# Values, gates and matrix memory as two stages, and the second modulation moved into the feature stages

## What is computed

```python
h = modulate(rmsnorm(x), shift, scale)          # shift, scale: 2 of 6 blocks of silu(c) @ ada_w + ada_b
P = h @ w_in                                    # RWKV, qk, values, i and f gates, ...
# mLSTM, per direction z (2), head (4) and chunk, state C, n, m:
b = cumsum(fc); m_new = max(b_end + m, max(b_end - b + ic))
C = exp(b_end + m - m_new) * C + sum_s w_end[s] * v[s] k[s]^T
s = (q @ k.T) * exp(log_d - m_row)              # log_d masked: causal within the chunk
h = (s @ v + a_inter * C q) / max(|den|, exp(-m_row))
y = sum over z of h * rsqrt(mean(h^2)) * norm_g
# then RWKV-7 (features, scan) for context and latent tokens, merge, experts
```

## Time and profile before

| | us |
|---|---|
| median of 3 runs (lowest, highest) | 3045.11 (3043.85, 3045.47) |
| the profiled execution: its time, its span | 3045.84, 3044.1 |
| values stage, gates stage, mLSTM stage | 75.0, 83.1, 170.0 |
| context features, latent features | 34.9, 53.8 |
| PE busy in the span | 2727.3 (90%) |
| granted clock in the span | 0.924 |

### The profile page before, as it was taken

The page is one execution under the profiler, slowest core; times in us unless marked ns, Lnnn a source line. Parts: engine busy times, 40 slices in busy tenths (PEclk is TensorE's granted clock), DMA queues, the critical chain, the costliest instruction groups (busy, mean ns, idle before and its releaser), DMA issues. The chain is left out here.

```text
span 3044.1 us, 54577 instructions
## 1 busy us (share of the span) xinstructions
PE 2727.3 (90%) x20260; PEld 2215.5 (73%) x20260; DVE 1279.3 (42%) x2767; ACT 1043.2 (34%) x1778; POOL 779.4 (26%) x641
## 2 busy tenths in 40 slices
PE   5798899678599959969978999997999999999998
PEld 2684268476499748748857888886888888888886
DVE  1221313454655533228994444442003444444443
ACT  2221113424333422233215666663223222222222
POOL 0520100032244224334445555552441000000000
PEclk9899965589799979989998999998999999999999
DMA  4220410000000033223323554455444555555552
GB/s 169 83 62 31 173 56 1 7 1 9 2 0 0 5 111 96 90 82 115 100 66 122 186 196 162 174 208 199 145 144 169 193 193 192 193 193 193 193 192 80
DMA packets 159929, 349.08 MB, mean 115 GB/s; under 512 B 13224, under 2 KB 79272, under 8 KB 156528
## 3 DMA queue, kind: packets, MB, share of 16 engines
q1 hardware_dynamic: 159856, 348.10, 33.3%
HBM read 276.75 MB, written 71.30 MB: 114 GB/s over the span
## 5 line engine op out<-in xcount | busy, mean ns | idle before, releaser
L85 PE MATMUL ps_a<-h_hi,u_hi 128*128 128x512 f32 x1024 | 407.1, 398 | 23.3 <-PEq L105 16.6
L86 PE MATMUL ps_a<-h_hi,u_lo 128*128 128x512 f32 x1024 | 400.9, 391 | 0.0
L87 PE MATMUL ps_a<-h_lo,u_hi 128*128 128x512 f32 x1024 | 400.4, 391 | 0.0
L2389 DVE TENSOR_TENSOR v_lo<-v_raw,v_hi 128x1024 fp32r<-128x1024 f32 x128 | 158.2, 1236 | 564.5 <-ACT v_hi L2347 564.4
L85 PE MATMUL ps_y<-gated_hi,v_hi 128*128 128x512 f32 x768 | 299.6, 390 | 3.1 <-DVE gated_lo L2391 3.1
L2347 ACT ACTIVATE v_hi<-v_raw 128x1024 fp32r<-128x1024 f32 x128 | 135.8, 1061 | 478.1 <-PE ps_a L87 469.7
L87 PE MATMUL ps_y<-gated_lo,v_hi 128*128 128x512 f32 x768 | 299.4, 390 | 0.0
L86 PE MATMUL ps_y<-gated_hi,v_lo 128*128 128x512 f32 x768 | 299.3, 390 | 0.0
L85 PEld LDWEIGHTS ps_a<-h_hi,u_hi 128*128 128x128 f32 x1024 | 193.9, 189 | 62.4 <-issue 23.0
L87 PEld LDWEIGHTS ps_a<-h_lo,u_hi 128*128 128x128 f32 x1024 | 193.5, 189 | 40.9
L86 PEld LDWEIGHTS ps_a<-h_hi,u_lo 128*128 128x128 f32 x1024 | 193.8, 189 | 37.9
(11 more groups left out here) (473 smaller groups left out, 5653.1 us busy)
## 6 DMA issues: line engine op xcount, KB each, us to landing
u_raw<-in_uT SPq DMA_DIRECT2D x128, 512.0 KB, 3.6
v_raw<-in_v SPq DMA_DIRECT2D x128, 512.0 KB, 4.8
a_scratch<-act SPq DMA_DIRECT2D x128, 256.0 KB, 2.2
w_scratch<-w_block SPq DMA_DIRECT2D x8, 4096.0 KB, 12.1
w_ring<-w_scratch SPq DMA_DIRECT2D x64, 512.0 KB, 4.4
gated<-a_scratch SPq DMA_DIRECT2D x128, 256.0 KB, 4.8
ada_ring<-in_ada_w SPq DMA_DIRECT2D x12, 2048.0 KB, 7.6
mg_raw<-in_w_merge SPq DMA_DIRECT2D x36, 512.0 KB, 3.5
```

Source lines behind the costliest of these rows:

```text
L85: pe.matmul(out, wh, xh, start=first, stop=False)
L86: pe.matmul(out, wl, xh, start=False, stop=False)
L87: return pe.matmul(out, wh, xl, start=False, stop=last)
L2389: v.tensor_tensor(vl[:, q], v_raw[:, q], vh[:, q], ALU.subtract).then_inc(v_lo, 1)
```

## The change

- The gates stage is gone. `phase_values` now loads the gate weights first, multiplies both kinds of gates in one product of 100 columns (`F_ROW` = 64), and runs the gate chain on DVE and ACT while PE makes four value tiles; the turning of the rows stands between the fourth and the fifth tile.
- `phase_mlstm` works on two heads a unit (8 context units, 16 latent ones). Scores are made once for both directions, 512 wide; the exponents are 512 wide; keys are turned once for both directions. In the first part, per head, these stand beside the context units; in the second only three pairs of products stand in a unit. Half of the queries-by-state pair uses array rows 0 to 63, half 64 to 127; half of the keys-by-values pair makes output rows 0 to 63, half 64 to 127. The sum of squares goes from DVE to ACT, in blocks of 8 instructions a chunk, and one direction's last scaling to POOL.
- The 8 modulation tiles go to the feature stages: 3 with the context, 5 with the latent tokens, after the norm's sums, which now wait for all of ACT's reads of the four banks they share. ACT copies the first tile's row ahead of the norm's Ln.
- h of the latent tokens is kept in `mixed` (`b.acc`), so some instructions of the modulation stage that were 768 wide are now 512 and 256; POOL's two adds a tile in the projection become one copy.
- The semaphores are cleared once more, behind the mLSTM.

```diff
+MOD_SECOND = MOD_FIRST + 3
...
+                for s, part in enumerate((xx[:, j], h[:, j, TX:])):
+                    m = act.activation(part, part, ACT.Identity, bias=b.mod[:, j, s:s + 1])
                 m.then_inc(shifted, 1)
                 act.wait_ge(shifted, j + 1)
-                act.activation(b.hh[:, j], h[:, j], ACT.Copy).then_inc(rounded, 1)
+                act.activation(b.hh[:, j, 0:TX], xx[:, j], ACT.Copy)
+                act.activation(b.hh[:, j, TX:], h[:, j, TX:], ACT.Copy).then_inc(rounded, 1)
...
-        ps = [ctx.enter_context(nc.psum_tensor(f"ps_rf{k}" + tag, [P, 512], F32)) for k in range(8)]
+        ps = [ctx.enter_context(nc.psum_tensor(f"ps_rf{k}" + tag, [P, 512], F32)) for k in range(4)]
+        mod = Modulation(nc, ctx, a, b, "_2" + tag, lo, hi, sb("mod_row" + tag, [2, hi - lo, MOD_W]), 3)
...
+            mod.load_bias(sp)
+            for n in range(n_mod):
+                mod.load(sp, n)
...
+            mod.copy_row(act, 0)
...
             pe.wait_ge(sq_done, 1)
+            pe.wait_ge(a_done, 2 * PAIRS)
             for c in range(PAIRS):
-                mm = pe.matmul(ps[4 + c][:, 0:T], b.block_ones[:], tmp[:, c, :], start=True, stop=True)
+                mm = pe.matmul(ps[c][:, 0:T], b.block_ones[:], tmp[:, c, :], start=True, stop=True)
             mm.then_inc(norm_mm, 1)
+            for n in range(n_mod):
+                mod.multiply(pe, n)
+            mod.turn(pe)
...
+        def _(pe):
+            pe.wait_ge(w_in, 16)
+            for j in range(KT):
+                pe.matmul(ps_x[0:F_ROW + GROWS, :], wg[:, j, :], b.h[:, j, 0:TX], start=(j == 0), stop=(j == KT - 1))
+            for j in range(KT):
+                mm = pe.matmul(ps_c[0:F_ROW + GROWS, 0:TC], wg[:, j, :], b.h[:, j, TX:],
+                               start=(j == 0), stop=(j == KT - 1))
+            mm.then_inc(g_mm, 1)
+            pe.wait_ge(v_in, 16)
+            def value(t):
...
+                for j in range(KT):
+                    mm = pe.matmul(ps_v[t % 2][:], b.h[:, j, t * MC:(t + 1) * MC], wv[:, j, :], start=(j == 0), stop=(j == KT - 1))
+                mm.then_inc(v_mm, 1)
+            for t in range(early_v):
+                value(t)
+            pe.wait_ge(rows_done, 1)
+            for n in range(NCH):
+                for k in range(4):
+                    o = (n * 2 + k % 2) * GROWS
+                    tr = pe.transpose(ps_t[k // 2][:, o:o + GROWS], turn[:, k, n * MC:(n + 1) * MC], ident[:])
+            tr.then_inc(t_done, 1)
+            for t in range(early_v, n_v):
+                value(t)
...
+                act.wait_ge(v_mm, t + 1)
+                act.activation(b.vM[:, t, :, 0:DV], ps_v[t % 2][:].rearrange("p (h v) -> p h v", v=DV),
+                               ACT.Copy).then_inc(v_out, 1)
+            for t in range(2):
+                evict(t)
             act.wait_ge(want[1], 1)
+            act.activation(rows[:, 4], rows[:, 4], ACT.Exp).then_inc(act_done, 1)
             act.activation(rows[:, INTER], rows[:, INTER], ACT.Exp).then_inc(act_done, 1)
             act.activation(rows[:, FLOOR], rows[:, FLOOR], ACT.Exp, scale=-1.0).then_inc(act_done, 1)
-            act.activation(rows[:, 4], rows[:, 4], ACT.Exp).then_inc(act_done, 1)
-            for n in range(2, n_mod):
-                mod.copy_row(act, n)
+            for t in range(2, n_v):
+                evict(t)
...
+            def scores(h):
+                j, lo = h // 2, h % 2 * DQK
+                if h < 2:
+                    pe.wait_ge(kc_done, 2)
+                else:
+                    pe.wait_ge(p_done, 2 * (h - 1))
+                for i in range(n_x):
+                    t = slice(i * MC, (i + 1) * MC)
+                    mm = pe.matmul(ps_s[h % 2][:, t], b.qX[lo:lo + DQK, HP + j, t], b.qX[lo:lo + DQK, j, t],
...
+            def exponent(h, z):
+                n = 2 * h + z
+                out = ps_e[(n + 1) % 2]
+                if n == 0:
+                    pe.wait_ge(kept, 1)
+                elif n % 4 == 1:
+                    pe.wait_ge(kx_done, n // 4 * 2 + 2)
+                    if n > 1:
+                        pe.wait_ge(exp_done, (n - 1) * n_x)
+                else:
+                    pe.wait_ge(exp_done, (n - 1) * n_x)
+                wide = mask[:, z].unsqueeze(1).to_broadcast([P, n_x, MC])
+                pe.matmul(out[:].rearrange("p (n t) -> p n t", t=MC), b.ident[:], wide, start=True, stop=False)
+                pe.matmul(out[:], select[:, z * MH + h, :], b.neg_m[:], start=False, stop=True).then_inc(e_mm, 1)
...
+                v0 = chunk if latent else n_x + chunk
+                kw = (kw_x if latent else kw_c)[:, z, j, chunk]
+                if latent:
+                    t = slice(chunk * MC, (chunk + 1) * MC)
+                    if i == 0:
+                        pe.wait_ge(p_done, 2 * (2 * j + 1) + z + 1)
+                    if n >= per:
+                        pe.wait_ge(c_done, n - per + 1)
+                    for p in range(2):
+                        pe.matmul(ps_u[k][:, p * W:(p + 1) * W], pw[:, z, 2 * j + p, t], b.vM[:, v0, 2 * j + p, :],
                                   start=True, stop=True)
-                    else:
-                        act_s.wait(pe, 0, f"kt{w}")
-                    pe_s.mark(pe.matmul(ps[k][:, FRESH_AT:FRESH_AT + DV + 1], ktw[:, k], vv, start=True, stop=True))
+                    if n > first_x:
+                        pe.wait_ge(hi_done, n - first_x)
+                    for p in range(2):
+                        lo = p * DQK
+                        pe.matmul(ps_i[p][:, 0:W], b.qX[lo:lo + DQK, j, t],
+                                  mC[lo:lo + DQK, 2 * j + z, :], start=True, stop=True)
+                    if i == 0:
+                        pe.wait_ge(kx_done, 2 * j + z + 1)
+                else:
+                    pe.wait_ge(kc_done, 2)
+                for p in range(2):
+                    lo = p * DQK
+                    mm = pe.matmul(ps_u[k][lo:lo + DQK, FRESH:FRESH + W], kw[:, lo:lo + DQK], b.vM[:, v0, 2 * j + p, :],
+                                   start=True, stop=True)
+                mm.then_inc(unit_mm, 1)
...
+            pe.wait_ge(small_in, 48)
+            for h in range(MH):
+                scores(h)
+                if h % 2 == 0:
+                    turned_keys(h // 2)
+                for z in range(2):
+                    exponent(h, z)
+                    unit(2 * h + z)
+            for n in range(first_x, last):
+                unit(n)
             for n in range(n_x):
                 pe.wait_ge(summed, n + 1)
                 for h in range(MH):
...
+            def inter(n):
+                latent, i, j, z = units[n]
+                chunk = chunk_of(n)
+                act.wait_ge(unit_mm, n + 1)
+                for p in range(2):
+                    m = act.activation(hc[:, z, chunk, 2 * j + p], ps_i[p][:, 0:W], ACT.Copy,
+                                       scale=cols(COL_INTER, n_c + chunk, z, slice(2 * j + p, 2 * j + p + 1)))
+                m.then_inc(hi_done, 1)
+            def squares(i):
+                for z in range(2):
+                    chunk = i if z == 0 else n_x - 1 - i
+                    act.wait_ge(den_done, 2 * i + z + 1)
+                    for h in range(MH):
+                        if i or z or h:
+                            act.wait_ge(sq_done, i * 2 * MH + z * MH + h)
+                        act.activation(junk[:], hc[:, z, chunk, h, 0:DV], ACT.Square, scale=dn[:, z, chunk, h:h + 1],
+                                       accum_out=ssq[:, z, chunk, h:h + 1]).then_inc(sq_done, 1)
...
+            for h in range(MH):
+                exponents(h)
+            for i in range(n_x):
+                for n in range(first_x + per * i, first_x + per * (i + 1)):
+                    inter(n)
+                if i:
+                    squares(i - 1)
+            squares(n_x - 1)
+            act.wait_ge(sq_done, n_x * 2 * MH)
             act.activation(ssq[:], ssq[:], ACT.Ln, bias=b.eps[:, 0:1], scale=1.0 / DV).then_inc(rooted, 1)
             act.wait_ge(rooted, 1)
...
+            b.clear_semaphores(nc)
...
+                phase_rwkv_features(nc, a, b, b.fC, TC, "_c", MOD_FIRST, MOD_SECOND)
                 phase_rwkv_scan(nc, a, b, b.fC, TC, "_c", False)
-                phase_rwkv_features(nc, a, b, b.fX, TX, "_x")
+                phase_rwkv_features(nc, a, b, b.fX, TX, "_x", MOD_SECOND, MOD_TILES)
```

More of the change, by code:

```diff
@@ L589, in _ @@
             act.activation(tmp[:], tmp[:], ACT.Exp, scale=-0.5).then_inc(norm_root, 1)
+            for n in range(1, n_mod):
+                mod.copy_row(act, n)
         @block.tensor
@@ L1303, in phase_mlstm @@
-        small_in, rooted, summed, turned, dve = (sem(f"mls_{n}") for n in ("in", "root", "sum", "turned", "link"))
-        def in_order(*stages):
-            names = []
-            for s in range(last + 5):
-                for back, name, latent in stages:
```

(35 more changed lines are left out.)

504 lines of the change are left out of this document (225 added, 279 removed).

## The result

The changed kernel takes 2974.51 us (median of 4 runs, 2973.03 to 2979.59) against 3045.29 for the kernel before beside it: a ratio of 0.9771, 95% interval 0.9754 to 0.9788. That is faster, as forecast, by 71 us and not by 129: the time lies outside the range of 2893 to 2943. The profiled execution is the longest of the four (span 2977.3 us), so spans are compared with spans.

What follows compares the result with a forecast made beforehand. Limits taken: PE in values, modulation beside the gate chain, half-speed PE in the mLSTM, ACT then DVE in feature stages. 97.0 + 61 - 16.0 - 9.3 - 1.6 - 1.5 = 129.6 us less, giving 2916.2; range 2893 to 2943.

Steps and rivals of the forecast that it cites:

- small terms: Outside the main stages: clearing 1.6 us more, modulation stage 1.5 more, POOL's fewer adds and PE's scan start nothing.
- PE's start in the scans: nothing: Both scans: no change in time, since PE comes from idle or the turning, at half speed either way.
- Values and gates: Values and gates stages: 97.0 us less, gate chain hidden by value tiles, mLSTM starting at 316.7 instead of 413.7.
- Rival 4: Values stage: gate chain not hidden, PE standing before the turned rows; 2926 us at worst, chance 0.03.
- mLSTM: mLSTM stage: 109 us against 170.0, 61 less, summed from 6.2, 30, 58 and 14.8.
- the first part: mLSTM, four heads' scores, exponents, context units and turned keys at full speed, with slow start: 30 us.
- units and squares: mLSTM: sixteen latent units at half speed, 2.6 us each, plus exposed ACT squares: 58 us together.
- Rivals 1 and 2: mLSTM: half speed throughout, adding 16 us, 2934, chance 0.17; full speed throughout, units saving 14, 2900, chance 0.15.
- Rival 3: mLSTM units: output-split pair runs one after the other, adding 8.6 us, 2925; chance 0.13.
- Rival 5: mLSTM: units cannot overlap through `ps_i`, taking 10.7 us each; 3046 us and more, slower than before; chance 0.01.
- the clearing: Semaphore clearing behind the mLSTM: 1.6 us more.
- Feature stages: Context and latent feature stages: 9.3 and 16.0 us more from modulation tiles on PE, ended by the turning.

Runs made afterwards that it cites:

- e4: All 32 mLSTM squares on ACT moved behind the last unit, against the changed kernel with 41 inserted instructions (2904.7 us): 2902.45 us.

## Why the prediction was wrong

**The step that failed** is a sentence of the small terms: "PE's start in the scans: nothing". I priced the scans by whether their products would start slow, and not by where their code lies, so that a stage whose code is the same was taken to last as long; no rival had it either. The sum made a span of 2914.5 (3044.1 less 129.6); measured were 2977.3. Of these 62.8 us the latent scan is 70.0, and the other terms together err by 7 the other way. With the place of before given back and nothing else changed, the kernel takes 2904.7, inside the range. Two other errors partly cancel in that: the mLSTM is 14.2 us shorter than forecast, mostly by a clock that I had wrong, and the feature stages and the context scan are 9.7 us longer. Neither alone would leave the range. The Trainium skill, "Runtime: NRT & Kernel Launch", Instruction fetch mechanics, says that an engine's instruction memory is filled in blocks of 256 instructions and that a taken branch whose target isn't in the current window of two blocks forces a fetch and a stall; I did not weigh it. The trace agrees with the mechanism: 68 packets in the scan in place of 13, and waits "for issue" at L831. It doesn't agree with two blocks: in the kernel before the loop jumps back over 6.8 blocks in every round, and most rounds move no packet. The same section of the Trainium skill gives PE 2048 instructions, eight blocks; by that alone the 1,730 of the body would stay from any place, and the runs show that they don't always.

**Values and gates: 97.0 forecast, 97.9 measured.** PE starts at 258.9 (259.3), its turned rows stand at 299.5 (300.0) without a wait, the mLSTM starts at 316.5 (316.7). Rival 4 is out: these rows of PE's timeline have no idle time before L1149.

```profile
258.86 9.81 PE L1129 MATMUL ps_gx<-h_f,win_gates 128*100 128x512 f32 x16 [7.73 <-DMA win_gates<-in_w_gates]
268.51 3.62 PE L1131 MATMUL ps_gc<-h_f,win_gates 128*100 128x256 f32 x16
271.96 27.63 PE L1140 MATMUL ps_pv<-win_v,h_f 128*128 128x512 f32 x64
299.52 1.68 PE L1149 MATMUL ps_gt<-gate_ident,gate_turn 36*128 36x36 f32 x24
```

**mLSTM: 109 forecast, 94.8 measured.** The start took 4.6 us (6.2), the first part 27.2 (30), from the first scores at 321.10 to the first latent unit at 348.25. The mis-sized term is units and squares: 58 forecast, 45.2 measured, up to the table load at 393.41. I took half speed for all sixteen units; nine and most of a tenth ran at full speed; the units are 10.4 of the 12.8 us missed. My 1.7 and 2.6 us for a unit were near (1.59 and 2.52). Rivals 1 and 2 both put the clock down to the kind of products; it was the stop behind ACT, as e4 shows. A square took 0.53 us (0.6), the first eight held PE for 3.1 and the second for 1.7 (2.9 each), and the last two blocks took 8.6 (9.6). Rival 3 is out: the output-split pair (L1401 to L1387) takes 0.62 us at half speed, where one after the other would take 0.86 without any change of layout; taken as 0.43 side by side, it leaves 0.19 for the layout. Rival 5 needed 10.7 us a unit. From the squares to the next stage's start it was 17.9 us against 14.8 and 1.6 for the clearing; the 1.5 left over were not traced.

**Feature stages: 9.3 and 16.0 forecast, 12.6 and 19.8 measured.** The tiles ran at 6.9 us, as taken, with 0.8 to 1.0 of wait for a load in place of 0.7. In the latent stage the norm's sums start 23.0 us behind its start (20.6 in the earlier trace rows and 2.7 were forecast), but take 6.4 in place of the 3.7 of the earlier trace rows; they end 2.3 us late, the tiles with their waits take 0.7 more and what follows them 0.8 more, which makes the 3.8 us missed. In the context stage the same three are 1.1, 0.8 and 1.4 us, which makes 3.3.

```profile
606.96 6.42 PE L543 MATMUL ps_rf_x<-rw_tmp_x,block_ones 128*128 128x512 f32 x8 [2.78 <-ACT qa L518]
613.31 13.89 PE L155 MATMUL ps_row_x<-ada_ring_x,silu_c 128*2 128x512 f32 x32
```

Both stages end with the turning and not with DVE, as forecast. The context scan's 2.6 were not in the sum. It moves 12 packets of instructions in both kernels, so it isn't hit as the latent scan is; its granted clock is 0.93 in place of 0.95. More was not tested.

## What to carry to other kernels

Where a loop's body is as long as this one, the time can depend on where in a block the body lies, so that any edit ahead of it can cost or give 7 to 13 us a round. Before a change in one stage is judged, compare the untouched stages too, and look at the instruction queue's packets and the waits "for issue" in the loop; if they have grown, shift the loop by some tens of harmless instructions (0.15 us each here) and time it again before judging the change. And where short products run at full speed, look for the wait that will stop them: a stop of 3.1 us also made the six units behind it 0.9 us longer each.

## What the runs showed of the hardware

- A loop body of 1,730 PE instructions isn't fetched again with its end at places 142, 163 and 184 of 256 (29.2 us a round). At 205, 225 and 250 it is in two, three and four rounds, at 122 in all six that follow a jump back. A round that is hit moves nine packets of 16,384 bytes and takes 36 to 42 us.
- 129-column products in pairs, one pair behind the other, ran on at a granted clock of 1.00 through all sixteen units; where a stop of 3.1 us came inside the tenth, the rest ran at 0.50.
- A row of semaphore increments on PE that nobody waits for is not free: each takes 0.15 us (8.1 us of idle with 41, 35.0 with 215), and 215 of them put the scan 25.8 us back.
- An ACT square with its sum is two instructions in the trace, 0.40 and 0.19 us, one every 0.53.
